# Projecting both later parts of the tokens in the first gather stage of a hybrid block kernel

## What is computed

```python
h = rmsnorm(x, norm_mix_w)
proj = h @ w_in                      # z, x/B/C, dt | q/k/v, gate, beta, alpha
ssd = ssd_chunked(silu(causal_dwconv(xbc) + b), dt, ...)      # 8 heads of 64
gdn = gated_delta_chunked(silu(causal_dwconv(qkv)), ...)      # 4 heads of 128
x = x + concat(rmsnorm(ssd * silu(z)), rmsnorm(gdn) * silu(gate)) @ w_out
hf = rmsnorm(x, norm_ffn_w)
q = hf @ w_q                         # 8 heads, 2 halves of 128
scores = q . sub_keys                # 16 lists of 128 scores for each token
s1, i1 = top_k(scores[:, :, 0], 16); s2, i2 = top_k(scores[:, :, 1], 16)
top_s, top_c = top_k(s1[:, None] + s2[None, :], 16)
idx = i1[top_c // 16] * 128 + i2[top_c % 16]     # 128 experts for each token
act = gelu(hf . u_tab[idx]) * softmax(top_s)
x = x + sum(act * v_tab[idx])
out = rmsnorm(x, norm_final_w)
```

## Time and profile before

| | us |
|---|---|
| median of three runs | 3428.85 |
| time of the profiled execution | 3437.05 |
| its span, first to last instruction | 3435.3 |
| TensorE busy | 2539.3 (74%) |
| VectorE busy | 2073.3 (60%) |
| GpSimd busy | 1975.4 (58%) |
| ScalarE busy | 561.3 (16%) |
| read from DRAM, over the span | 1159.82 MB, 345 GB/s |

### The profile page before, as it was taken

One profiled execution on the slowest core, in us unless ns is written; L12 is line 12 of the kernel. 1 busy time (PEld: TensorE's weight loads), 2 busy tenths in 40 slices (PEclk: granted clock), 3 DMA queues, 4 the chain that ended last, 5 costly groups with the idle time before them and its releaser, 6 DMA issues.

```text
span 3435.3 us, 27404 instructions
## 1 busy us (share of the span) xinstructions
PE 2539.3 (74%) x9080; PEld 1040.8 (30%) x9080; DVE 2073.3 (60%) x4704; ACT 561.3 (16%) x1160; POOL 1975.4 (58%) x2097
## 2 busy tenths in 40 slices
PE   6876389847887678867888577857885878566698
PEld 5763265414331243213431142113211421111121
DVE  3343676887575666766575677667766776544300
ACT  3341144412121212112110110011001100000000
POOL 1100233345566556666666677767776777777775
PEclk8988699969999899998999899989998999898999
DMA  5530477889999999999999999999999999999998
GB/s 153 195 133 1 167 245 263 295 323 349 339 385 364 377 334 382 388 393 360 367 381 356 407 394 409 407 408 388 409 409 407 400 409 408 409 409 409 409 404 354
DMA packets 356957, 1185.38 MB, mean 345 GB/s; under 512 B 41984, under 2 KB 73104, under 8 KB 356560
## 3 DMA queue, kind: packets, MB, share of 16 engines
q0 software_dynamic: 297072, 1079.97, 81.2%
q1 hardware_dynamic: 58592, 99.47, 8.5%
q10 hardware_dynamic: 1152, 4.19, 0.3%
HBM read 1159.82 MB, written 23.66 MB: 345 GB/s over the span
## 4 chain that ended last, share of the span: by engine, by line
POOL 24%; DMA 24%; PE 22%; DVE 13%; issue 10%; ACT 2%; SPq 0%; DVEq 0%; ACTq 0%; POOLq 0%
POOL ring L869 24%; DMA ring<-in_peer_v_dram,picks_T 14%; DMA ring<-in_peer_u_dram,picks 9%; PE y_psum L946 7%; DVE ring L1319 4%; PE b_bank L901 3%; PE y_psum L901 2%; PE tile_psum L1099 2%; PE tile_psum L1078 2%; DVE arena L1552 1%; DVE arena L1556 1%; PE tile_psum L1040 1%; DVE arena L1559 1%; PE tile_psum L1041 1%; PE tile_psum L1022 1%
## 5 line engine op out<-in xcount | busy, mean ns | idle before, releaser
L946 PE MATMUL y_psum<-ring,spread 128*32 128x512 f32 x4096 | 1359.9, 648 | 517.5 <-DMA ring<-in_peer_v_dram,picks_T 516.3
L1319 DVE CUSTOM_DVE_ANT_0 ring<-ring,h_psum 128x1024 f32<-128x1024 f32 x1024 | 1236.3, 1218 | 809.2 <-DMA ring<-in_peer_u_dram,picks 795.1
L869 POOL DMA_INDIRECT ring<-in_peer_u_dram,picks x1024 | 972.7, 950 | 864.9 <-DVE dots L1319 267.9
L869 POOL DMA_INDIRECT ring<-in_peer_v_dram,picks_T x1024 | 969.5, 947 | 431.5 <-issue 261.2
L946 PEld LDWEIGHTS y_psum<-ring,spread 128*32 128x32 f32 x4096 | 263.4, 114 | 1501.5 <-DMA ring<-in_peer_v_dram,picks_T 890.1
L1099 PE MATMUL tile_psum<-w_q,arena 128*128 128x512 f32 x512 | 224.9, 597 | 1.1 <-ACT arena L1275 1.1
L1178 ACT COPY spread<-zero 128x8 f32<-128x8 f32 (+1 forms) x104 | 21.6, 208 | 861.2 <-PE y_psum L946 861.1
L901 PE MATMUL b_bank<-ring 128*128 128x384 f32 (+1 forms) x464 | 156.0, 490 | 0.0
L1099 PEld LDWEIGHTS tile_psum<-w_q,arena 128*128 128x128 f32 x512 | 97.0, 191 | 122.8 <-issue 119.4
L1078 PE MATMUL tile_psum<-w_out,arena 128*128 128x512 f32 x256 | 120.9, 617 | 1.1 <-ACT arena L1262 1.1
L1347 DVE SCALAR_TENSOR_TENSOR res<-res,stat_e,final_row 128x1024 f32<-128x1024 f32 x8 | 10.3, 1283 | 176.7 <-ACT stat_e L1195 176.7
(11 more groups left out here) (242 smaller groups left out, 2351.0 us busy)
## 6 DMA issues: line engine op xcount, KB each, us to landing
ring<-in_w_units_dram SPq DMA_DIRECT2D x42, 512.0 KB, 6.4
ring<-in_peer_u_dram,picks POOLq DMA_INDIRECT x1024, 7.8
ring<-in_peer_v_dram,picks_T POOLq DMA_INDIRECT x1024, 8.5
w_blk<-in_w_units_dram SPq DMA_DIRECT2D x28, 512.0 KB, 4.0
ring<-in_w_q_T_dram SPq DMA_DIRECT2D x16, 512.0 KB, 3.5
res<-in_w_units_dram SPq DMA_DIRECT2D x14, 512.0 KB, 5.7
arena<-tok_scr SPq DMA_DIRECT2D x8, 768.0 KB, 9.2
arena<-zgs_scr SPq DMA_DIRECT2D x8, 520.0 KB, 21.8
```

Source lines behind the costliest of these rows:

```text
L869: pool.indirect_dma_start(ring[:, j], None, tables[kind], bass.IndirectOffsetOnAxis(ap=at, axis=0)).then_inc(filled[j], 16)
L946: last = nc.tensor.matmul(y_ps[quad * STEPS:(quad + 1) * STEPS, half], lines[:, quad, at:at + STEPS], ring[:, j, half * BANK:(half + 1) * ...
L1319: nc.vector.tensor_tensor_reduce(out=ring[:, j], in0=ring[:, j], in1=h_ps[:], scale=1.0, scalar=0.0, op0=ALU.mult, op1=ALU.add, accum_out= ...
```

## The change

- `UNITS_OF` puts all 58 later units into gather stage 0. Stages 1 to 3 have none, so the ring has its 11 slots from stage 1 on (`FEW_STAGES` is 1 in place of 4). All units use two banks, two halves of `final_row` and two weight slots in turn.
- `with_units` cuts a unit's products into four pieces half a gather apart; Q comes with the last piece, K and Z two gathers after the begin, D and Y 4.2 gathers after it (before: products at once, K and Z two gathers and D and Y five gathers after the begin in stage 0).
- Front stage: x is loaded into eight buffers (in the room of w_q) without a wait, ScalarE computes the eight factors before the first unit, three tiles (5 to 7) are turned between the units and the other three (2 to 4) after the last. The taps and the bias come as one laid-out transfer on SP's queue. w_out is loaded earlier and multiplied by its norm weights here, not in the prologue. Five slots of w_q's weights are loaded before the barrier.
- Steps of a tile: x is turned and multiplied by w_q without its factor (`h2` is gone), and the factor is applied in the copy of the scores. ScalarE's square no longer stands ahead of the transposition.
- Search: in the prologue and in stage 0 each bank's four lists are searched as soon as the bank is copied. The chosen ids are made by rank in place of by head: the first eight ranks of all heads are compared with the 20 candidates that can hold them, the others with all 50.

```diff
-UNITS_OF = {0: (0, UNITS)} | {1 + n: (UNITS + UNITS * n // 3, UNITS + UNITS * (n + 1) // 3) for n in range(3)}
+UNITS_OF = {0: (0, LATE)}
...
+FEW_RUNS = [(a, TOPK // 2 // (a + 1)) for a in range(TOPK // 4)]
+FEW_AT = [sum(n for _, n in RUNS[:a]) + b for a, n in FEW_RUNS for b in range(n)] + [sum(n for _, n in RUNS[:a]) for a in range(TOPK // 4, TOPK // 2)]
+FEW_CANDS = len(FEW_AT)
...
+PIECES = 4
...
-    begin, gap = (1, 2) if e == 0 else (16, 5)
+    begin, taps, turn = 1, 2, 4.2
     points = []
     for n in range(first, to):
-        at = begin + (total - begin - 3 * gap) * (n - first) // (to - first)
-        points += [(at, n, "BQ"), (at + gap, n, "KZ"), (at + 2 * gap + (e == 0), n, "DY")]
+        at = begin + (total - begin - turn - 3) * (n - first) / (to - first)
+        points += [(at + j / 2, n, (f"B{j}",)) for j in range(PIECES)]
+        points += [(at + (PIECES - 1) / 2, n, "Q"), (at + taps, n, "KZ"), (at + turn, n, "DY")]
...
+        late = w_q[:].rearrange("p k c -> p (k c)")
+        x_in, x_sq = view(late[:, 0:TILES * D], TILES, D), late[:, TILES * D:(TILES + 1) * D]
+        hn = [sb("hn_first", [P, KD, FIRST]), part["hn"], view(late[:, (TILES + 1) * D:(TILES + 1) * D + KD * PART], KD, PART)]
...
+        ORDER = [*range(FIRST_TILES), *range(FIRST_TILES + PART_TILES, TILES), *range(FIRST_TILES, FIRST_TILES + PART_TILES)]
+        BETWEEN = FIRST_TILES + PART_TILES
         def norm_after(u):
-            return FIRST_TILES + u // 3 if u % 3 == 1 and u < 3 * (TILES - FIRST_TILES) else None
+            return FIRST_TILES + u // 3 if u % 3 == 1 and u < 3 * PART_TILES else None
...
-                if i >= 2:
-                    sp.wait_ge(norm_turned, i - 1)
-                sp.dma_start(x_in[:, i % 2], x_rows[i]).then_inc(x_loaded[i % 2], 16)
+                sp.dma_start(x_in[:, i], x_rows[i]).then_inc(x_loaded[i], 16)
...
+            sp.dma_start(part["conv"][:, 0:TAPS * BLOCKS + SSD_BLOCKS], A["conv"]).then_inc(conv_consts_loaded, 16)
...
-                tile = norm_after(u - W_BUFS)
-                if tile is not None and tile + 2 < TILES:
-                    load_x(tile + 2)
-                if u >= UNITS - 2 * KD and u % 2:
-                    k = (u - (UNITS - 2 * KD)) // 2
-                    sp.dma_start(w_out[:, k], w_out_src[:, k]).then_inc(w_late_loaded, 16)
+                if u >= W_BUFS + 2 and u % 2 == 0 and u < W_BUFS + 2 + 2 * KD:
+                    k = (u - W_BUFS - 2) // 2
+                    sp.dma_start(w_out[:, k], w_out_src[:, k]).then_inc(w_out_loaded, 16)
...
+            for l in range(FOLD_SLOTS):
+                sp.dma_start(ring[:, l], A["w_q_T"][l]).then_inc(wq_loaded[l], 16)
...
+            for i in range(BETWEEN, TILES):
+                turn_x(i)
...
-            for i in range(FIRST_TILES):
+            for i in range(TILES):
                 rms(i)
-            act.wait_ge(conv_consts_loaded, 16 * CONV_CONSTS)
+            act.wait_ge(conv_consts_loaded, 16)
...
-                tile = norm_after(u + 1) if u + 1 < UNITS else None
-                if tile is not None:
-                    rms(tile)
...
+            dve.wait_ge(w_out_loaded, 16 * KD)
+            dve.wait_ge(consts_loaded, 16 * N_CONST)
+            for k in range(KD):
+                nc.vector.tensor_scalar(w_out[:, k], w_out[:, k], fixed["w_mix"][:, min(k, 4):min(k, 4) + 1], None, ALU.mult)
+            for i in range(BETWEEN, TILES):
+                scale_x(i)
+            for i in range(BETWEEN, TILES):
+                weigh(i)
...
-        b_late = sb("b_late", [P, PART])
...
-                    if n < UNITS - 2 or n >= UNITS - 1:
-                        load_unit(n + 2 if n < UNITS - 2 else n + 1)
+                    load_unit(n + 2)
...
-                if kind == "B":
-                    pe.wait_ge(*loads_of(n))
-                    if n == 0:
-                        pe.wait_ge(s["wq_copied"], len(FOLDS))
-                    if n >= UNITS:
-                        pe.wait_ge(s["hn_loaded"], 16)
-                        pe.wait_ge(s["b_silu"], n)
-                        pe.wait_ge(s["b_framed"], LATE_TURNED[n])
-                    elif n >= 2:
-                        pe.wait_ge(s["b_silu"], n - 1)
-                    for k in range(KD):
+                if kind[0] == "B":
+                    piece = int(kind[1])
+                    if piece == 0:
+                        pe.wait_ge(*loads_of(n))
+                        if n == 0:
+                            pe.wait_ge(s["wq_copied"], len(FOLDS))
+                        if n >= UNITS:
+                            pe.wait_ge(s["hn_loaded"], 16)
+                        if n >= 2:
+                            pe.wait_ge(s["b_silu"], n - 1)
+                    for k in range(KD // PIECES * piece, KD // PIECES * (piece + 1)):
                         last = nc.tensor.matmul(unit_bank(n)[0:unit_width(n), HALO:HALO + PART], unit_weights(n)[:, k], hn[:, k], start=(k == 0), stop=(k == KD - 1))
-                    last.then_inc(s["b_proj"], 1)
+                    if piece == PIECES - 1:
+                        last.then_inc(s["b_proj"], 1)
...
-                pe.wait_ge(s["h2_ready"], m + 1)
+                pe.wait_ge(s["x2_ready"], m + 1)
                 for k in range(KD):
-                    last = nc.tensor.transpose(square(0, 2)[:, k], h2[:, k * P:(k + 1) * P], ident[:])
+                    last = nc.tensor.transpose(square(0, 2)[:, k], x2[:, k * P:(k + 1) * P], ident[:])
...
-                nc.scalar.activation(h2, x2[:], ACT.Copy, scale=stat[:, 5:6]).then_inc(s["h2_ready"], 1)
-                share()
...
-                    nc.scalar.copy(score[:, 4 * b:4 * (b + 1)], square(SCORE_BANKS[b])).then_inc(s["score_copied"], 1)
+                    nc.scalar.activation(score[:, 4 * b:4 * (b + 1)], square(SCORE_BANKS[b]), ACT.Copy, scale=stat[:, 5:6]).then_inc(s["score_copied"], 1)
...
-                    if isinstance(m, int) and m == 0 and n < 5:
-                        dve.wait_ge(w_late_loaded, 16 * KD)
-                        for k in (2 * n - 2, 2 * n - 1):
-                            nc.vector.tensor_scalar(w_out[:, k], w_out[:, k], w_mix[:, min(k, 4):min(k, 4) + 1], None,
-                                                    ALU.mult).then_inc(s["w_out_ready"], 1)
...
+                if m < 2:
+                    groups = [(range(4 * b, 4 * (b + 1)), 2 if b == 3 else None, lambda b=b: scored(b, 2)) for b in range(4)]
+                else:
+                    groups = [(range(LISTS), 8, lambda: scored(3, 9))]
...
-                full = [P, HALF_H, TOPK, CANDS]
                 nc.vector.tensor_copy(rank_ps, rank[:]).then_inc(s["chosen_ready"], 1)
                 dve.wait_ge(s["chosen_ready"], 3 * m + 1)
-                for half in range(2):
-                    hs = slice(half * HALF_H, (half + 1) * HALF_H)
+                for half, (ids, ranks) in enumerate(((few_id, rank_ps[:, CANDS:]), (cand_id, rank_ps[:, 0:CANDS]))):
+                    ks, chosen = slice(half * n8, (half + 1) * n8), chosen_of[half]
+                    full = list(chosen.shape)
```

## The result

The changed kernel took 3464.9 us (median of four runs, 3464.6 to 3472.8), the kernel before 3428.7 beside it: a ratio of 1.0101, 95% interval 1.0081 to 1.0122. It is **slower by 36 us**, where 28 us less were forecast.

What follows compares the result with a forecast made beforehand. It took the early part as bound by chains of engines and waits, later stages by transfers, slowed by units in stages 1 to 3. Terms -34 - 29 + 174 - 139 = -28 off the median gave 3401 us, range 3335 to 3442.

Steps and rivals of the forecast that it cites:

- Front stage, -34: Front stage: earlier first units, fewer norms between units, a longer end; 34 us less, range 27 to 38.
- Prologue, -29: Prologue: weights loaded ahead, shorter chain to x's transposition, search by bank, shorter passes; 29 us less, range 22 to 31.
- Stages 1 to 3, -139: Stages 1 to 3: without units each takes stage 4's 341.9 us; 139 us less, 43 as the other end.
- The third rival: Stages 1 to 3 stay at 370 GB/s: 43 us gained in place of 139, time 3497; chance 0.05.
- Stage 0, +174: Stage 0 with all 58 units: 491 us of units plus begin, reload and end, sum 539; 174 us more than 364.9.
- 2.6 at 550 to 640: Stage 0: stores land after 2.6 us, as in that stretch of the earlier trace, giving a convolved unit 8.5 us.
- The weights: Stage 0: load waits behind Y(n); two units take landing, products and issues, 16.8 us, so 8.4 a unit.
- TensorE term: Stage 0: products 5.8 us, transpositions 0.5 and steps 1.4 a segment make 7.7 a unit, 9.7 beside a projection.
- In stage 0 the same edits: Stage 0: the prologue's edits lie beside TensorE's work, later beside the transfers, and gain nothing.
- The second: Stage 0: store cycle with landings of 4.5 us, 235 us more, time 3462, 33 us slower; chance 0.22.
- the first: Stage 0: TensorE alone sets it, the pieces hide the landings; 486 us, 121 more, time 3348; chance 0.22.
- The table loads: Stage 0: each costs 1.28 us without the skill's drain; with it about 110 us longer, near 3510; chance 1 in 50.

Runs made afterwards that it cites:

- run 8: Changed kernel with the gathers of stages 1 to 3 kept on seven ring slots in place of eleven, no units there: 3533.9 us, ratio 1.028.
- Runs 3: Changed kernel with SyncE issuing the load of unit n+3's weights ahead of the store of unit n in stage 0: 3417.4 us, ratio 0.9969.
- run 4: Changed kernel with a third buffer for the units' sums, so ScalarE waits for an older store: 3468.1 us, ratio 1.0105.
- Run 6: Changed kernel with both the load ahead of the store and a third buffer for the sums: 3355.2 us, ratio 0.9771.
- runs 1: Changed kernel with D and Y placed 4.0 gathers behind a unit's first products in place of 4.2: 3381.6 us, ratio 0.9856.
- 5: Changed kernel with D and Y at 4.1 gathers in place of 4.2, so D moves ahead on TensorE but Y stays: 3451.6 us, ratio 1.0055.
- run 2: Changed kernel with the units' placing undone, 29 in stage 0 and 29 over stages 1 to 3, products in one piece: 3346.2 us, ratio 0.9760.
- run 16: Kernel of run 2 with tile 1's search, in stage 0, put back to one pass behind the last bank: 3355.7 us, ratio 0.9787.
- 14: Kernel of Run 6, unchanged, run again on a chip with slower transfers: 3652.7 us, ratio 0.9943.
- first eight experiments: Edits to the changed kernel's unit placing, D and Y, load order, sum buffers and ring slots: 3346.2 to 3533.9 us.
- next seven: Variants and repeats of the kernels of run 2 and Run 6, on a chip with slower transfers: 3579.9 to 3652.7 us.
- the last: The same as run 16: 3355.7 us, ratio 0.9787.

## Why the prediction was wrong

- **Front stage, -34:** right, a little low. It gave up 36.1 us (178.85 to 142.72; the earlier trace rows); the third unit began at 27.31 (29.5 forecast).
- **Prologue, -29:** right, 29.1 in all. From SyncE's first load to the sum in x it is 4.2 less (6 forecast, with w_out), from there to the end of the search 19.5 (17.2 forecast), from there on 5.5 (5.6 forecast).
- **Stages 1 to 3, -139:** right in size (150). "Without units they have stage 4's work and its 11 slots" names both causes and prices them as one; run 8 parts them, 53 for the slots and 95 for the units. The sentence that it could be less "only if what slows them were not the units" had a third of it wrong. The third rival, 370 GB/s, did not come: 402 to 407.
- **Stage 0, +174:** this is the step that failed: 251. The period of a unit, forecast at 8.47, was 10.05, which is 92 us over 58 units; the end, forecast at 20.5, was 5, since the dots and passes lay under the last units, and gave 15 back. What the list of cycles had wrong:
  - "2.6 at 550 to 640 ... the same density, so I take the landings of the earlier trace rows." Those were the lowest at hand: over the whole stage before, `tok_scr` stores took 4.2 and the loads 6.3 and 5.7. Nor did density decide: 236 GB/s at 550 to 640 us before, 188 in the whole stage after. Stores landed after 4.0, which alone makes the stores' cycle 5.4 + 4.0 = 9.4; the loads, 5.2 and 5.0, were near the 4.9 assumed.
  - "The weights: ... 16.8, 8.4 a unit." It left out what stands between the pieces on TensorE: the steps' 1.4 a segment, which the prediction's own TensorE term has. With it, (16.8 + 2 x 1.4)/2 = 9.8 is an estimate near the measured 10.05; that this is where the time went is argued. It also left out a cycle of one unit, load, first piece, D, Y, load, which the rows from 897.48 show at 6.7. Runs 3, 4 and 6 show that the weights' chain ruled; runs 1 and 5 that Y(n)'s place behind the next SiLU made it long (70 us), and D's place little (13).
  - "In stage 0 the same edits lie beside TensorE's work ...: nothing there." They were worth 20 us with 29 units (run 2; 8.7 of them tested, run 16), where VectorE's list ended that stage. This hides in the 251: the units' price was 270.
- **The rivals.** The second gave 3462 and the cause "the store cycle". The number came true, by luck in part: run 4 takes that cycle away and gains nothing, and runs 3 and 6 show it as the shorter of two. Run 6 comes near to the first (TensorE alone, 486 us in stage 0, 3348): 505 us and 3355.
- **The table loads.** Each load began within 0.02 us of the SiLU's end (496.32 after 495.69 + 0.62), as in the earlier trace rows. Taking 97 of them away shortened stage 0 by 10 us. The Trainium skill (ScalarE: Activation LUTs, What ACT_TABLE_LOAD costs) gives a load 1283 ns, which the rows have, and a drain of about 1380 ns more at each switch, which no row here shows.
- **The sum.** -65.2 + 250.7 - 150.2 + 0.2 in the later stages = +35.5 on the span. Had stage 0 been 539, the time would have been 3388. The range's upper end, 3442, was too low: it stopped short of a rival that had 0.22.

The best kernel found is run 2: front stage, prologue and search as changed, units placed as before, 3346 us, and its ratio of 0.976 held on both chips.

## What to carry to other kernels

When a chain of loads and stores passes through several in-order engines, write out whose instruction each one waits behind, and look for the copy that both a store and the next load need. If two cycles come out within an us of each other, an experiment must open both: here one alone showed 0 or 48 us of a gain of 110. Take the time to landing over the whole stage, and not over its best 90 us. And price a stage's work against the engine that ends that stage, not against the one that is busiest in the whole program: the same number of units, 29, cost 270 us in a stage bound by latency and 148, ring slots included, in stages bound by transfers, and only 91 there when the transfers were slow.

## What the hardware showed unasked

Whole gather stages on eleven slots and without units ran at 402 to 408 GB/s (DMA share 1.02 to 1.03) in the first eight experiments, at 349 to 367 GB/s (0.92 to 0.97) in the next seven, for all kernels alike, and at the higher pace again in the last. The kernel before took 3429 to 3434 us at the one and 3666 to 3668 at the other. The mean granted TensorE clock of the profiled executions was 0.90 to 0.92 at the one and 0.87 to 0.89 at the other, and stage 0, bound by latency, stayed at 505 (runs 6 and 14). The Trainium skill (HBM Reference, Specifications) says that two cores share the bandwidth of a memory domain: about 425 GB/s for one that streams alone, about 358 each when both do. The two levels here are near these two figures; that a neighbour was at work is not shown, since no trace here sees one.
